# Exchanged row blocks and two moved steps in the seven-product FFN of a two-layer fp32 transformer kernel

## What is computed

```python
def _conv_ffn(h, w_up, conv_w, conv_b, w_down):     # h: tokens x 1024, w_up: 1024 x 5632
    u = h @ w_up
    up = jnp.pad(u, ((0, 0), (1, 1), (0, 0)))
    u = sum(up[:, i:i + T] * conv_w[i] for i in range(3)) + conv_b
    a, gate = jnp.split(u, 2, axis=-1)
    return (jax.nn.silu(gate) * a) @ w_down
...
    x = x + ga1 * _rmsnorm(mixed @ w_out, g_post_mix)
    h = _rmsnorm(x, g_pre_ffn) * (1.0 + sc2) + sh2
    x = x + ga2 * _rmsnorm(_conv_ffn(h, w_up, conv_w, conv_b, w_down), g_post_ffn)
```

## Time and profile before

| | |
|---|---|
| median of 3 runs | 1598.72 us (1597.17 to 1599.05) |
| the profiled execution's own time | 1599.95 us |
| its span, first to last instruction | 1598.1 us |
| PE busy | 1575.2 us, 99% |
| DVE busy | 1316.9 us, 82% |
| ACT busy | 781.8 us, 49% |
| POOL busy | 392.6 us, 25% |
| mean granted TensorE clock | 0.998 of full speed |

### The profile page before, as it was taken

The page is one execution under the profiler, slowest core; times in us unless marked ns, Lnnn a source line. Parts: engine busy times, 40 slices in busy tenths (PEclk is TensorE's granted clock), DMA queues, the critical chain, the costliest instruction groups (busy, mean ns, idle before and its releaser), DMA issues.

```text
span 1598.1 us, 28345 instructions
## 1 busy us (share of the span) xinstructions
PE 1575.2 (99%) x9688; PEld 1390.6 (87%) x9688; DVE 1316.9 (82%) x2295; ACT 781.8 (49%) x1443; POOL 392.6 (25%) x302
## 2 busy tenths in 40 slices
PE   8999999999999999999999999999999999999998
PEld 6787898789999999888878879977899999998886
DVE  7899788668999999976669987976689999998575
ACT  5433235538655565534383323273766565563333
POOL 0032034001445455200000600700035455541000
PEclk9999999999999999999999999999999999999999
DMA  9345365051222222454414444722312222335351
GB/s 369 122 133 163 97 249 182 15 145 54 66 82 89 79 91 79 144 172 158 151 41 145 135 136 157 253 79 82 78 62 84 79 92 79 92 92 174 129 185 66
DMA packets 66214, 195.05 MB, mean 122 GB/s; under 512 B 15441, under 2 KB 16849, under 8 KB 65873
## 3 DMA queue, kind: packets, MB, share of 16 engines
q1 hardware_dynamic: 50834, 175.54, 34.3%
q10 hardware_dynamic: 15296, 18.39, 3.5%
HBM read 187.05 MB, written 6.85 MB: 121 GB/s over the span
## 4 chain that ended last, share of the span: by engine, by line
PE 80%; DVE 10%; issue 4%; DMA 1%; ACT 1%; ACTq 1%; DVEq 0%; SPq 0%
PE bank L2120 12%; PE bank L2121 12%; PE bank L2122 12%; PE bank L2632 10%; PE bank L2634 10%; PE bank L2633 10%; DVE ada_sq L1370 2%; PE bank L2428 2%; DVE w_lo L1359 2%; PE bank L2414 1%; DMA raw<-in_stream 1%; PE bank L2492 1%; PE bank L2490 1%; PE bank L2488 1%; PE bank L2142 1%
## 5 line engine op out<-in xcount | busy, mean ns | idle before, releaser
L782 ACT ACTIVATE w_hi<-raw 128x1024 fp32r<-128x1024 f32 (+1 forms) x120 | 123.1, 1029 | 393.2 <-PE bank L2122 297.1
L1359 DVE TENSOR_TENSOR w_lo<-raw,w_hi 128x1024 fp32r<-128x1024 f32 (+1 forms) x128 | 156.4, 1229 | 106.7 <-ACT w_hi L782 106.2
L2120 PE MATMUL bank<-w_hi,aT_lo 128*128 128x512 f32 x520 | 210.6, 405 | 2.1 <-DVE aT_lo L1821 2.0
L2121 PE MATMUL bank<-w_lo,aT_hi 128*128 128x512 f32 x520 | 206.1, 396 | 0.0
L2122 PE MATMUL bank<-w_hi,aT_hi 128*128 128x512 f32 x520 | 205.6, 395 | 0.0
L2632 PE MATMUL bank<-aT_hi,w_lo 128*128 128x322 f32 x640 | 200.5, 313 | 4.5 <-DVE u L1986 4.5
L2633 PE MATMUL bank<-aT_lo,w_hi 128*128 128x322 f32 x640 | 200.0, 313 | 0.0
L2634 PE MATMUL bank<-aT_hi,w_hi 128*128 128x322 f32 x640 | 199.5, 312 | 0.0
L1257 ACT ACTIVATE w_hi<-raw 128x512 fp32r<-128x512 f32 x200 | 117.7, 626 | 105.4 <-POOL raw L664 105.4
L2120 PE MATMUL bank<-w_hi,m_lo 128*128 128x512 f32 x400 | 158.5, 396 | 0.0
L2121 PE MATMUL bank<-w_lo,m_hi 128*128 128x512 f32 x400 | 157.3, 393 | 0.0
(11 more groups left out here) (292 smaller groups left out, 3903.9 us busy)
## 6 DMA issues: line engine op xcount, KB each, us to landing
raw<-in_stream SPq DMA_DIRECT2D x304, 512.0 KB, 3.7
lead<-in_lead SPq DMA_DIRECT2D x16, 512.0 KB, 10.3
bias<-in_bias ACTq DMA_DIRECT2D x8, 896.0 KB, 10.8
na_v<-vn ACTq DMA_DIRECT2D x2, 1280.0 KB, 7.7
x<-in_xs SPq DMA_DIRECT2D x4, 512.0 KB, 12.0
vt<-na_v ACTq DMA_DIRECT2D x16, 128.0 KB
gb_mix<-gates ACTq DMA_DIRECT2D x2, 1024.0 KB, 4.5
gb_ffn<-gates ACTq DMA_DIRECT2D x8, 256.0 KB, 4.3
```

The costliest lines, as they stand in the source:

```text
L782: act.activation(w_hi[:, g % 4, 0:n], raw[:, s % 4, 0:n], ACT.Copy).then_inc(hi_done, 1)
L1359: dve.tensor_tensor(w_lo[:, g % 4, 0:n], raw[:, s % 4, 0:n], w_hi[:, g % 4, 0:n].bitcast(F32), ALU.subtract).then_inc(raw_free[s % 4], 1)
L2120: pe.matmul(out, ll, rh, start=start, stop=False)
L2121: pe.matmul(out, lh, rl, start=False, stop=False)
```

## The change

The two row blocks of tokens change places in the sums and products. S1 is now the sum over block 0, S2 subtracts part (1, 0), S3 is taken the other way round, and S4 starts from part (1, 1) and goes over part (0, 0). Products 0, 4, 5 and 6 take the other block, and `column_banks` names the result banks accordingly. S1 needs only tiles 0 to 2 now. DVE makes it after `mod_(3)`, ahead of tile 3's low part, and ACT rounds it (`s_high(0)`) after `hi(3)`, ahead of tile 4. S2 moves from behind tile 4's low part to ahead of it. On GpSimd the fourth sum gets one more wait, for ACT's half of tile 4. On DVE, `block_low(5, 1, 0)` and `block_low(6, 1, 0)` move from behind `gate_sum(1, 0)` to ahead of `first_with_sixth(1, 0)`.

```diff
-            return ((a_, b_), (d_, c_))[g] + (HZ,)
+            return ((b_, a_), (c_, d_))[g] + (HZ,)
...
                 pool.wait_ge(blk_lo, at(blk_lo, layer, 5))
-                pool.tensor_tensor(s_sum[:, 0], h_part(0, 1), s_sum[:, 1], ALU.subtract).then_inc(s_sum_done, 1)
+                pool.wait_ge(norm_mod2, at(norm_mod2, layer, 2 * NT))
+                pool.tensor_tensor(s_sum[:, 0], h_part(1, 1), s_sum[:, 1], ALU.subtract).then_inc(s_sum_done, 1)
...
                 mod_(3)
                 hi(3)
+                s_high(0, layer)
                 mod_(4)
                 hi(4)
...
-                s_high(0)
-                s_high(1)
+                s_high(1, layer)
...
                 mod_(3)
+                dve.wait_ge(norm_mod2, at(norm_mod2, layer, NT + 3))
+                dve.tensor_tensor(s_sum[:, 0], h_part(0, 0), h_part(0, 1), ALU.add).then_inc(s_sum_done, 1)
                 low(1, 3, layer)
                 mod_(4)
                 dve.wait_ge(norm_mod, at(norm_mod, layer, 2 * NT))
-                dve.wait_ge(norm_mod2, at(norm_mod2, layer, 2 * NT))
-                dve.tensor_tensor(s_sum[:, 0], h_part(1, 0), h_part(1, 1), ALU.add).then_inc(s_sum_done, 1)
+                dve.wait_ge(s_sum_done, at(s_sum_done, layer, 1))
+                dve.tensor_tensor(s_sum[:, 1], s_sum[:, 0], h_part(1, 0), ALU.subtract).then_inc(s_sum_done, 1)
                 low(1, 4, layer)
...
-                dve.wait_ge(s_sum_done, at(s_sum_done, layer, 1))
-                dve.tensor_tensor(s_sum[:, 1], s_sum[:, 0], h_part(0, 0), ALU.subtract).then_inc(s_sum_done, 1)
-                dve.tensor_tensor(s_sum[:, 2], h_part(0, 0), h_part(1, 0), ALU.subtract).then_inc(s_sum_done, 1)
+                dve.tensor_tensor(s_sum[:, 2], h_part(1, 0), h_part(0, 0), ALU.subtract).then_inc(s_sum_done, 1)
...
                 s_low(0)
-                block_low(3, 1, 0)
-                block_low(4, 1, 0)
+                for n in range(3, 7):
+                    block_low(n, 1, 0)
...
                 gate_sum(1, 0)
-                block_low(5, 1, 0)
-                block_low(6, 1, 0)
                 s_low(3)
...
-                        block_product(0, e, 0, *a_part(0, 0))
+                        block_product(0, e, 0, *a_part(1, 0))
...
-                        block_product(4, e, 0, *a_part(0, 1))
+                        block_product(4, e, 0, *a_part(1, 1))
...
-                        block_product(5, e, 1, *a_part(1, 1))
+                        block_product(5, e, 1, *a_part(0, 1))
...
-                        block_product(6, e, 3, *a_part(1, 0))
+                        block_product(6, e, 3, *a_part(0, 0))
```

More of the change, by code:

```diff
@@ L936, in half_squares, with s_high @@
                     tile_squares(w, n, tt, layer)
+            def s_high(n, layer):
+                dst = (s31_hi[:, 1], s2_hl[:, 0], s31_hi[:, 0], aT_hi[:, 0:HP, 0:HZ])[n]
+                act.wait_ge(s_sum_done, at(s_sum_done, layer, n + 1))
+                if n == 3:
+                    act.wait_ge(w_used, at(w_used, layer, W_UP0 + G_ONE))
+                act.activation(dst, s_sum[:, n % 3], ACT.Copy).then_inc(s_hi_done, 1)
             def turn_ffn(layer):
@@ L1236, in column_mid @@
                                    scale=tap(1, g, q, layer)).then_inc(tap_mid, 1)
-                def s_high(n):
-                    dst = (s31_hi[:, 1], s2_hl[:, 0], s31_hi[:, 0], aT_hi[:, 0:HP, HZ:TZ])[n]
-                    act.wait_ge(s_sum_done, at(s_sum_done, layer, n + 1))
-                    if n == 3:
-                        act.wait_ge(w_used, at(w_used, layer, W_UP0 + G_ONE))
-                    act.activation(dst, s_sum[:, n % 3], ACT.Copy).then_inc(s_hi_done, 1)
                 def block_high(n, i, e, first=False):
@@ L1279, in _ @@
                 column_mid(None, 0, 1)
-                s_high(2)
+                s_high(2, layer)
                 block_high(2, 1, 0, True)
@@ L1291, in _ @@
                 block_high(1, 1, 1)
-                s_high(3)
+                s_high(3, layer)
                 for n in range(2, 6):
@@ L1967, in s_low @@
                 def s_low(n):
-                    dst = (s31_lo[:, 1], s2_hl[:, 1], s31_lo[:, 0], aT_lo[:, 0:HP, HZ:TZ])[n]
-                    hi = (s31_hi[:, 1], s2_hl[:, 0], s31_hi[:, 0], aT_hi[:, 0:HP, HZ:TZ])[n]
+                    dst = (s31_lo[:, 1], s2_hl[:, 1], s31_lo[:, 0], aT_lo[:, 0:HP, 0:HZ])[n]
+                    hi = (s31_hi[:, 1], s2_hl[:, 0], s31_hi[:, 0], aT_hi[:, 0:HP, 0:HZ])[n]
                     dve.wait_ge(s_hi_done, at(s_hi_done, layer, n + 1))
```

## The result

The changed kernel takes 1603.52 us (median of 8 runs, 1602.33 to 1605.09), the kernel before 1598.43 beside it (8 runs, 1597.17 to 1599.35). The ratio is 1.003 with a 95% interval of 1.0021 to 1.004: slower by about 5 us, where 1599.6 was forecast and 1602.5 was the end of the range.

A forecast was written before the change was run, and what follows sets the result against it. PE was taken as the bound, busy 1575.2 us, 99% of the span. Exchange 0 and the fourth s_low 0.45 us later in each layer gave +0.9, so 1599.6 us from a median of 1598.72; range 1593.0 to 1602.5.

The forecast's parts named there:

- Same number of matmuls, same 322 columns, same banks ... : 0: Exchange of row blocks in PE's products: same matmuls, columns, banks and pairs of waits, so a cost of 0.
- I take 0: Port between DVE's parts 5 and 6: part 6, ready about 408.7, precedes gated's request about 410.1, so 0 added.
- the bound of 1.45: Most that part 6 could lose to gated on the shared port: gated's length less 0.13, 1.45 us.
- the row of 4.33: Earlier trace row at 664.61: gated took 4.33 us in place of 1.58 while two DVE splits kept the port.
- The hold of part 5: Part 5 on DVE, ready at 408.15, held by S4 until 410.07; fourth s_low 0.45 us later in each layer.
- S1 early: S1 in DVE's idle 2.37 us ahead of tile 3's low part: DVE 0.74 us earlier from the second column_conv.
- Rival 2: gated slips in between parts 5 and 6: 1.90 us lost per layer, 1602.5, or 1599.3 by the clock; chance 0.14.
- Rival 1: DVE isn't held: fourth s_low 1.20 us earlier, 1593.1 or 1596.3; chance 0.24, shared with S1 gaining nothing.
- The clock: After PE's 2.23 us without work in pair (1, 1), the stay at 1.2 GHz was to remain in both layers.
- the 1.62 of the prediction: Cost per layer of PE running two products at 1.2 GHz in pair (1, 1): 5.18 us in place of 3.56.

The follow-up runs named there:

- the parts alone: Kernel before with only block_low parts 5 and 6 moved ahead of the output sums: 1598.77 us against 1598.09, ratio 1.0007.
- the run with the parts put back: Changed kernel with parts 5 and 6 back behind gate_sum, exchange and early S1 kept: 1600.77 us against 1598.95, ratio 1.002.
- S4 behind both: S4 waits until part 6 is split: in the changed kernel 1598.72 us, ratio 1.0006; without the block exchange and early S1 1597.38 us, ratio 0.9991.
- the one with the new bank names: Kernel before with only column_banks naming the banks as in the changed kernel: 1600.32 us against 1598.95, ratio 1.0007.
- the last two: Kernel before, parts 5 and 6 early, S4 behind them; next iteration's low parts 1 and 0, or 0 alone, behind first_with_sixth: 1599.58 us (0.9997), 1599.61 us (1.0003).
- the exchange alone: Changed kernel with S1, its high part, S2 and parts 5 and 6 at their former places: 1602.95 us against 1598.09, ratio 1.0037.

## Why the prediction was wrong

- **"Same number of matmuls, same 322 columns, same banks ... : 0" failed.** This is the step that costs most. It is 0.067 us in each pair, 2.4 us in all: 0.04 to 0.045 from the operands of products 4 and 5, 0.025 to 0.03 from product 0's. Instruction counts and shapes were equal, and I never asked whether the place of an operand has a price. No row of before shows it.
- **"I take 0" for the port between parts 5 and 6 failed.** Part 6 took 2.06 us in place of 0.68, 1.38 against the bound of 1.45. The prediction counted part 6 as ready because it would be so at about 408.7, before `gated` asked, and so took the row of 4.33 for its case. That test fits its two rows, but so does another, and only the other fits what part 6 did: whether the next split's high half was there before the running DVE instruction started. In the earlier trace rows it was, since ACT's last high half ahead of the two splits ended at 661.93, and DVE kept the port. In the earlier trace rows it came 1.06 us after S1 had started, and GpSimd got the port. Part 5 was to start at 408.15, so a part 6 ready at 408.7 was the second kind by the prediction's own figures, and that is what came. The rival in which `gated` slips in had been given a chance of 0.14.
- **The hold of part 5 was right.** S4 was forecast at 407.46 and came at 406.82 (PE's products began 0.61 us earlier in this execution); part 5 was forecast at some 2.6 us and took 2.71. The hold ended 0.14 before the recorded end of S4, as the 0.13 of the earlier trace rows. So the Trainium skill's rule against the change ("SBUF — State Buffer", "Who interferes with whom") was the right one to weigh. Its sentence in the same section that issue order decides who blocks fits the changed kernel by the recorded starts (`gated` 409.52, part 6 410.04). It does not fit layer 1 of the parts alone (S4 1190.95, part 6 1191.29, and part 6 went first) or the earlier trace rows, so the measurement decides there.
- **S1 early was right in its mechanism and in its worth on DVE.** The second `column_conv` starts 1.45 us earlier, 0.84 when PE's own start is taken off, against 0.74. S1 itself took 2.27 in place of 2.10, and all fits in the idle time. It buys nothing in the end, as the run with the parts put back shows (29.51 us in the opening).
- **Rival 2 was priced right and given too small a chance.** It said 1.90 us in a layer, and 1.90 - 1.62 = 0.28 if the clock falls at the first wait. Layer 1 lost 1.91 and layer 0 lost 0.33. With the loop's 2.4 us this makes +4.6, against +5.1 for the medians.
- **Rival 1's benefit needs S4 behind both parts.** With S4 behind part 5 alone part 6 was held in one layer, and in the other S4 itself was, which brought 0.28 us. With S4 behind both, the opening gains 0.9 to 2.4 us a layer.
- **The clock** was taken to fall behind the wait of 2.23 us in both layers. It falls often, not always. Two equal pairs (1, 1) of one kernel (the one with the new bank names) took 16.50 and 14.98 us, the second with the clock up: 1.52 us, near the 1.62 of the prediction. In 14 kernels, all but the changed one and the last two, PE waited 1.8 to 2.3 us ahead of product 5 of (1, 1) in both layers; a fall followed in 19 of the 28. A difference of 1.5 us between two profiles can be this alone.

What stays open: why product 2 pays when product 0 reads row block 1, and product 5 when products 4 and 5 exchange their blocks, by a few nanoseconds in single matmuls. The block begins 322 x 4 = 1288 bytes into a row of `aT_hi` and `aT_lo`; whether that is the cause wasn't tried. Nor was the readiness of part 6 varied by itself. And it isn't settled why the median of the exchange alone lies 2.3 us above what its trace accounts for.

## What to carry to other kernels

Filling DVE's idle time with splits that read two SBUF operands was free here only where GpSimd read nothing in those microseconds. Look at what GpSimd starts there and behind it. Then ask of each split in the group whether its inputs are there before the one ahead of it starts; where they were not, GpSimd got in between. What worked was GpSimd's instruction behind the whole group. A change that is symmetric on paper (same counts, same shapes) still has to be measured on the repeated body: 0.5% of a loop that fills a quarter of the program took back 2.4 us of the 3.3 that the opening had won with S4 behind the parts. And where a wait of about 2 us is followed by a lower clock in some executions only, count the falls in each trace before reading a difference of 1.5 us as the effect of an edit.

## What the runs showed of the hardware

- The time of a chain of matmuls depends on where the moving operands lie. With clock, shape and banks equal, twelve matmuls of 322 columns (product 5) took 1.77 us, and 1.81 when products 4 and 5 had exchanged their row blocks; and product 2 went from 1.79 to 1.815 when only product 0's operand moved. The contents of the sums and the banks' names did not matter (pairs 12.44 with either changed).
- When GpSimd asks while DVE runs an instruction with two SBUF operands and another follows at once, either can be next. DVE kept the port in the 35 places where the next one's high half was there before the running one started (a `gated` of 4.33 us, an S4 of 3.64), and GpSimd got it in the 16 where it came later (2.06, 2.33 and 3.23 us for splits of 0.68, 1.23 and 0.68).
- The granted clock after equal waits is not reproducible: 2.09 us of idle time were followed by 0.50 in one layer and by 1.00 in the other. Behind waits of at most 1.7 us at this place it stayed up, in four layers, which are few.
